# Gate loads on ScalarE's own queue, row sums shifted by two, and a bank of its own for the last quarter of the last products

## The reference

```python
h = layer_norm(x)
z = h @ w_in                                   # pooled channels | q | k | v
mix = concat(pool_mixer(z), window_attention(z)) @ w_o
h = layer_norm(alpha * h + mix)
# product-key retrieval over 128*128 one-neuron experts, 8 heads, 16 picks each
a = einsum('td,thkd->thk', h, u_tab[idx])      # idx: 128 picked experts of a token
w = softmax_gates * gelu(a)
ffn = einsum('thk,thkd->td', w, v_tab[idx])
ple = sigmoid(h @ w_gate + b) * (p @ w_ple)
h = layer_norm(alpha * h + ffn + ple)
```

## Time and profile before

| | us |
|---|---|
| median of 3 runs (lowest, highest) | 1350.71 (1350.45, 1350.95) |
| the profiled execution: its own time | 1351.04 |
| its span, first to last instruction | 1349.1 |
| TensorE busy | 1325.6 |
| VectorE busy | 1158.7 |
| ScalarE busy | 658.0 |
| GpSimd busy | 572.4 |

### The profile page before, as it was taken

How to read it: one execution, slowest core, us unless ns; L and a number is a source line. 1 busy time by engine, 2 the same in 40 slices (tenths; PEclk the granted TensorE clock), 3 DMA queues, 4 the chain that set the end, 5 groups by cost and what they waited for, 6 DMA issues and landing times.

```text
span 1349.1 us, 23150 instructions
## 1 busy us (share of the span) xinstructions
PE 1325.6 (98%) x7689; PEld 719.4 (53%) x7689; DVE 1158.7 (86%) x2286; ACT 658.0 (49%) x928; POOL 572.4 (42%) x344
## 2 busy tenths in 40 slices
PE   6999999999999999999999999999999999999997
PEld 3554555546666666666655555555544444444443
DVE  8665579999988999999778888898998989988887
ACT  5552554546667676767543333343333433333341
POOL 2640233435553343434336666666663433322202
PEclk9999999999999999999999999999999999999999
DMA  7222222326577899999999999999999999999952
GB/s 294 94 79 94 79 94 78 110 78 184 183 235 234 338 375 366 359 376 373 395 337 368 350 374 352 361 399 362 371 365 383 386 391 391 385 389 377 362 185 97
DMA packets 148796, 384.51 MB, mean 285 GB/s; under 512 B 11776, under 2 KB 71424, under 8 KB 146560
## 3 DMA queue, kind: packets, MB, share of 16 engines
q1 hardware_dynamic: 111872, 249.54, 52.4%
q0 software_dynamic: 36864, 134.23, 25.7%
HBM read 340.74 MB, written 42.99 MB: 284 GB/s over the span
## 4 chain that ended last, share of the span: by engine, by line
PE 94%; DVE 3%; ACT 1%; issue 1%; DMA 1%; DVEq 0%; SPq 0%; ACTq 0%
PE bank L658 37%; PE bank L646 16%; PE bank L648 16%; PE bank L647 16%; PE bank L871 2%; PE bank L873 2%; PE bank L673 2%; PE bank L929 1%; PE bank L820 1%; PE bank L600 1%; PE bank L777 1%; PE bank L718 1%; PE bank L696 1%; DVE ple_gate L1766 0%; DMA norm_rows<-norms_dram 0%
## 5 line engine op out<-in xcount | busy, mean ns | idle before, releaser
L658 PE MATMUL bank<-cut,area 128*128 128x512 f16 x2208 | 483.2, 379 | 1.6 <-DVE cut L1324 1.6
L646 PE MATMUL bank<-hT,cut 128*128 128x384 f16 (+1 forms) x1232 | 413.0, 335 | 1.1 <-DVE cut L1324 0.5
L647 PE MATMUL bank<-hT,cut 128*128 128x384 f16 (+1 forms) x1232 | 412.8, 335 | 0.0
L648 PE MATMUL bank<-hT,cut 128*128 128x384 f16 (+1 forms) x1232 | 412.7, 335 | 0.0
L956 ACT ACTIVATE cut<-raw 128x1024 f16<-128x1024 f32 x246 | 256.0, 1054 | 204.5 <-PE bank L658 112.0
L658 PEld LDWEIGHTS bank<-cut,area 128*128 128x128 f16 x2208 | 215.9, 98 | 258.5 <-DVE cut L1324 2.5
L1324 DVE SCALAR_TENSOR_TENSOR cut<-raw,cut 128x1024 f16<-128x1024 f32 x198 | 248.1, 1254 | 63.0 <-ACT cut L956 61.6
L1173 ACT ACTIVATE gelu_out<-bank 128x384 f32<-128x384 f32 x120 | 59.0, 491 | 246.0 <-PE bank L648 246.0
L646 PEld LDWEIGHTS bank<-hT,cut 128*128 128x128 f16 x1232 | 120.6, 98 | 93.4 <-DVE hT L1446 3.0
L582 POOL DMA_INDIRECT ple_sb<-u_rows_dram,expert_id x64 | 112.3, 1755 | 135.6 <-DVE dots_now L1673 103.1
L648 PEld LDWEIGHTS bank<-hT,cut 128*128 128x128 f16 x1232 | 120.6, 98 | 90.9 <-issue 0.3
(11 more groups left out here) (190 smaller groups left out, 1552.3 us busy)
## 6 DMA issues: line engine op xcount, KB each, us to landing
raw<-tiles_dram SPq DMA_DIRECT2D x298, 512.0 KB, 6.4
gates_scratch<-area SPq DMA_DIRECT2D x12, 2048.0 KB, 11.7
area<-gates_scratch SPq DMA_DIRECT2D x32, 768.0 KB, 9.5
gelu_scratch<-gelu_out SPq DMA_DIRECT2D x80, 192.0 KB, 4.9
area<-gelu_scratch SPq DMA_DIRECT2D x20, 768.0 KB, 10.9
norm_rows<-norms_dram SPq DMA_DIRECT2D x3, 1024.0 KB, 5.9
hn<-x_dram SPq DMA_DIRECT2D x4, 512.0 KB, 4.9
out_dram<-hn SPq DMA_DIRECT2D x3, 512.0 KB, 2.6
```

The lines of the kernel that those rows point to most:

```text
L646: nc.tensor.matmul(dst, w[0], hT[:, 0, k, 0:width], start=(k == 0), stop=False)
L647: nc.tensor.matmul(dst, w[0], hT[:, 1, k, 0:width], start=False, stop=False)
L648: last = nc.tensor.matmul(dst, w[1], hT[:, 0, k, 0:width], start=False, stop=(k == KD - 1))
L658: mm = nc.tensor.matmul(bank[:, 2 * tt + h, :], lhs(a)[:, tt * P:(tt + 1) * P], cut[:, t.slot, b, h * HALF:(h + 1) * HALF], start=(first a ...
```

## The change

Four edits:

1. The gate loads of `both` and `late` leave SyncE's program. ScalarE issues them, on a queue of its own, right behind the cut of the weight whose making frees the buffer. The first two gate loads stay with SyncE. SyncE's `load_gelu` gets the wait (on `weight_done`) that the gate load ahead of it had.
2. `EIGHT_SUMS` goes from (24, 24) to (26, 22): e = 3 adds two rows more, e = 4 two less.
3. `light = 2` for e = 4: its first six passes keep three row adds each, its last two have two each.
4. The second half of the last token tile's last products is done as two quarters, the fourth in bank 6 (`2 * ND`), started afresh there. VectorE adds all of bank 5 after the third quarter (what bank 5 holds for the fourth from earlier tiles with it), then 256 columns of bank 6, with statistics of 512, 256 and 256 columns in `last_stats`.

```diff
-EIGHT_SUMS = (24, 24)
+EIGHT_SUMS = (26, 22)
+LAST_PIECES = ((2 * ND - 2, 0, HALF), (2 * ND - 1, HALF, HALF // 2), (2 * ND, HALF + HALF // 2, HALF // 2))
...
@@ SyncE, both(e) @@
-                    if p % 4 == 2:
-                        s = p // 4
-                        if isinstance(e, int) and e == EIGHTS - 1:
-                            load_gates(2 * e + 2 + s, VG * s, s)
-                        else:
-                            load_gates(2 * e + 2 + s, U_EARLY + VG * (2 * e + 2 + s), s)
@@ SyncE, late(e) @@
-                        load_gates(2 * EIGHTS + 2 * e + s + 2, VG * (2 * e + s + 2), s)
+                        sp.wait_ge(weight_done, N_BOTH + VG * (2 * e + s + 1))
                         load_gelu(2 * e + s + 2, s)
@@ TensorE, the last products of the last token tile @@
-            for h in range(2):
+            for piece in LAST_PIECES:
                 for i in range(2 * RING):
-                    mm = last_products(i, ND - 1, (h,))
+                    mm = last_products(i, ND - 1, (piece,))
                 mm.then_inc(experts_done, 1)
@@ ScalarE @@
+            def load_gates(group, first, parity):
+
+                act.wait_ge(weight_done, VG * (group - 1))
+                nc.scalar.dma_start(gates_in[:, parity],
+                                    gates_dram[:, :, bass.ds(first, VG), :].rearrange("c p e t -> p c e t")
+                                    ).then_inc(gates_loaded[parity], 16)
...
                         for w in ((i + 1, i + 2) if i == N_BOTH - 2 else (i + 2,)):
                             weight_high(w, w % RING, v_tile(w - RING))
+                        if p == 6:
+                            load_gates(2 * e + 3, VG, 1)
...
                     weight_high(i + 1, (p + 1) % RING, None if no_use else v_tile(i + 1 - RING))
+                    if p == 2 and isinstance(e, int) and e == EIGHTS - 1:
+                        load_gates(2 * e + 2, 0, 0)
+                    elif p % 4 == 2:
+                        load_gates(2 * e + 2 + p // 4, U_EARLY + VG * (2 * e + 2 + p // 4), p // 4)
...
+                    if v % 4 == 1 and (not fixed or 2 * e + v // 4 + 2 < N_LATE // VG):
+                        load_gates(2 * EIGHTS + 2 * e + v // 4 + 2, VG * (2 * e + v // 4 + 2), v // 4)
@@ VectorE, both(e, step, steps, light=0) @@
-                step_at = [steps * q // 8 for q in range(9)]
+                early = steps - 2 * light
+                step_at = [early * q // (8 - light) for q in range(9 - light)]
+                step_at += [early + 2 * (q + 1) for q in range(light)]
@@ VectorE, the end @@
-            for h in range(2):
-                dve.wait_ge(experts_done, 3 + h)
-                final_half(2, h)
-                final_stats(3, h)
-                if h == 0:
+            for n, (into, begin, count) in enumerate(LAST_PIECES):
+                dve.wait_ge(experts_done, 3 + n)
+                evicted = HALF if n < 2 else count
+                sums_n = hn[:, ND - 1, begin:begin + evicted]
+                nc.vector.scalar_tensor_tensor(out=sums_n, in0=bank[:, into, 0:evicted],
+                                               scalar=1 / (S_G * S_V * ALPHA), in1=sums_n, op0=ALU.mult,
+                                               op1=ALU.add).then_inc(final_sum, 1)
+                dve.wait_ge(final_sum, 2 * 3 + n + 1)
+                own.mark(nc.vector.bn_stats(last_stats[:, 6 * n:6 * n + 6], hn[:, ND - 1, begin:begin + count]))
+                if n == 0:
```

More of the change, by code:

```diff
@@ L191, in layer @@
         gate_b_row = sb("gate_b_row", [P, D])
+        last_stats = sb("last_stats", [P, 6 * len(LAST_PIECES)])
         stats = sb("stats", [P, TT, 12])
@@ L923, in _, with last_products, both_halves @@
             first_weight = N_BOTH + N_LATE - 2 * RING
-            def last_products(i, tt, columns_now):
+            def last_products(i, tt, pieces):
                 for step, (a, b) in enumerate(((0, 0), (0, 1), (1, 0))):
-                    for h in columns_now:
-                        mm = nc.tensor.matmul(bank[:, 2 * tt + h, :],
+                    for into, first, count in pieces:
+                        mm = nc.tensor.matmul(bank[:, into, 0:count],
                                               weight_halves(first_weight + i, i % RING)[:, a, tt * P:(tt + 1) * P],
-                                              halves_of(last[i])[:, b, h * HALF:(h + 1) * HALF],
-                                              start=False, stop=(i == 2 * RING - 1 and step == 2))
-                return mm
+                                              halves_of(last[i])[:, b, first:first + count],
+                                              start=(into == 2 * ND and i == 0 and step == 0),
+                                              stop=(i == 2 * RING - 1 and step == 2))
+                return mm
+            def both_halves(tt):
+                return ((2 * tt, 0, HALF), (2 * tt + 1, HALF, HALF))
             for group in (range(RING), range(RING, 2 * RING)):
@@ L1774, in _, with both @@
             weight_low(0, 0)
-            def both(e, step, steps):
-                step_at = [steps * q // 8 for q in range(9)]
+            def both(e, step, steps, light=0):
+                early = steps - 2 * light
+                step_at = [early * q // (8 - light) for q in range(9 - light)]
+                step_at += [early + 2 * (q + 1) for q in range(light)]
                 for p in range(8):
@@ L1810, in both_dots, with both_sums @@
                 keep_dots(first, count)
-            def both_sums(e, first, count):
+            def both_sums(e, first, count, light):
                 weights_now(first, count)
-                both(e, lambda j: add_row(j, first + j, first // ROW_RING + j // ROW_RING), count)
+                both(e, lambda j: add_row(j, first + j, (first + j) // ROW_RING, (first + j) % ROW_RING), count,
+                     light)
             first = U_GATES + KEPT_DOTS
@@ L1832, in _ @@
             for n, count in enumerate(EIGHT_SUMS):
-                both_sums(len(EIGHT_DOTS) + n, first, count)
+                both_sums(len(EIGHT_DOTS) + n, first, count, 2 if n == len(EIGHT_SUMS) - 1 else 0)
                 first += count
@@ L1855, in final_moments @@
                 own.settle()
-                own.link(nc.vector.bn_aggr(moments[:, t, :], stats[:, t, :]))
+                own.link(nc.vector.bn_aggr(moments[:, t, :], last_stats[:] if i == 3 else stats[:, t, :]))
                 nc.vector.tensor_scalar(v, moments[:, t, 1:2], EPS / ALPHA ** 2, None, ALU.add).then_inc(stats_done, 1)
```

19 lines of the change are left out of this document (8 added, 11 removed).

## The result

| | before | after |
|---|---|---|
| median of the runs | 1350.88 us (1350.45 to 1351.45, 6 runs) | 1360.65 us (1355.89 to 1365.53, 6 runs) |
| profiled execution, its span | 1351.04, 1349.1 us | 1363.67, 1361.8 us |

The ratio is 1.0074, 95% interval 1.0063 to 1.0085. The change makes the kernel about 10 us slower. The profiled execution is one of the slower of the six, so its trace shows 12.7 us more than before. The forecast was 1348.5 us, and the range up to 1350.6 doesn't hold the time. The rival "gates starve on their own queue" had 0.11.

What follows compares the result with a forecast made beforehand. TensorE was taken to bound the kernel, busy 1325.6 of 1349.1 us. The terms -1.76 - 0.09 - 0.40 = -2.25 us took the median from 1350.71 to 1348.5 us; range 1347.6 to 1350.6.

Steps and rivals of the forecast that it cites:

- gates starve on their own queue: Rival: gate loads beside two full queues land late; at 20 us to landing, 6.0 us lost, 1354.5 us; chance 0.11.
- the cost of nothing: Moving gate loads to ScalarE: 0.38 us of issue saved on SyncE each time, worth nothing on the path.
- It took 11.2 us before: 1003.3: Pass 6 of `both(4)`: gate load issued at 992.1 lands at 1003.3, 1.1 us before its use in `late`.
- four turns, 13 us or more: All gate loads except that of pass 6 in `both(4)`: each has four turns, 13 us or more, to land.
- bound of 14 us for the load of pass 6: Gate load of pass 6 in `both(4)`: a landing up to 1006.1, 14 us after issue, stalls nobody.
- Edits 2 and 3, -1.76: TensorE's stall at 1004: two fewer row adds bring VectorE's cut 2.78 us forward, winning 1.76 us.
- That rival's own two cases, 1.1 and 1.8 us: Rival, stall moves to a transfer in `late`: late gates lose 1.1 us, late gelu 1.8; 1349.0 to 1350.3; chance 0.22.
- The -0.09: Matmuls behind the stall at 1004: a hidden 0.09 us won, as the stored gelu is issued and lands sooner.
- Edit 4, -0.40: Tail behind the last matmul: splitting the last half into quarters starts the joining of statistics sooner, winning 0.40 us net.
- + 0.06: Tail: 48 matmuls of 256 columns take 5.24 us instead of 5.18 for 24 of 512, costing 0.06 us.
- The third stall: TensorE near 1323, 0.63 us: forecast to stay, as VectorE waits for norm rows; chance 0.12 that it goes, giving 1347.8.

Runs made afterwards that it cites:

- experiment 1: The changed kernel with the gate loads back on SyncE, row adds and last quarter as changed; 1348.41 us, ratio 0.9979.
- experiment 2: The kernel before with the gate loads issued by ScalarE and nothing else changed; 1364.39 us, ratio 1.0091.
- experiment 3: The changed kernel with ScalarE's gate loads reading 768 KB in runs of 6 KB, always from one place; 1348.23 us, ratio 0.9977.
- experiment 4: The changed kernel with ScalarE's gate loads in runs of 1 KB, always the same bytes; 1348.52 us, ratio 0.9975.
- experiment 5: The changed kernel with ScalarE's gate loads in runs of 256 bytes, always from one place; 1379.32 us, ratio 1.0204.
- experiment 6: The changed kernel with half of each gate load issued by SyncE and half by ScalarE, in runs of 512 bytes; 1348.58 us, ratio 0.9979.
- experiment 7: The kernel before with the row-add changes alone (26 and 22 rows, last two turns light); 1348.72 us, ratio 0.9982.
- exp. 8: The kernel before with only the last products' fourth quarter in a bank of its own; 1350.17 us, ratio 0.9994.
- exp. 12: The changed kernel with the gate loads back on SyncE, run once more on another chip; 1348.00 us, ratio 0.998.
- exp. 9: The changed kernel with gate loads back on SyncE and norm rows loaded ahead of the last tile loads; 1348.16 us, ratio 0.9978.

## Why the prediction was wrong, point by point

**Edit 1, the step that failed.** "It took 11.2 us before: 1003.3": the working took the landing of a load from a queue that it was to leave, and the cost of nothing followed from that. The one load that it worked out harmed nobody: it landed 13.7 us after its issue, and it could take 14. Its cover was indeed the thinnest. (Why it landed so much sooner than the loads before and behind it isn't known.) The others were passed over with "four turns, 13 us or more". The next of them took 23.6 us; VectorE could have borne 16.5 of that and TensorE 19.4 (23.6 less the 4.2 that it lost). In `both`, before any stall, nine loads (issued between 700 and 985) took 12.8 to 29.8 us, and TensorE lost nothing, since 31 us lie between two of them there; in `late` it is 15.5, four tiles of TensorE, where nothing stalls. Experiments 1 and 2 show the whole loss in this edit. Experiments 3 to 6 show its reason, the number of runs of one load in a queue beside two full ones:

| runs for each DMA engine, their size | landing, us (median, longest) | median of those in 700:985 | time, us |
|---|---|---|---|
| 8 of 6 KB | 8.0, 10.0 | 9.1 | 1348.23 |
| 48 of 1 KB | 13.1, 19.8 | 17.9 | 1348.52 |
| 48 of 512 bytes (half of a load) | one at 15.6 | not in the trace | 1348.58 |
| 96 of 512 bytes (the change) | 15.2, 29.8 | 22.6 | 1360.65 |
| 192 of 256 bytes | 42.1 the longest in the chain | not in the trace | 1379.32 |

The last column but one compares best. Behind the first stall the change's landings go up and down, from 24.8 us to 6.7, and that pulls its median down.

Could rows have given the size? Roughly. In 1066:1190 a packet of q1 lasts 0.449 x 16 x 124 / 5359 = 0.166 us, one of q0 in the same way 0.149 and one of q10 0.029. A run that waits for a packet of the tile queue alone takes 0.195, and of both 0.344, so 96 runs take 18.7 to 33 us, as an estimate; measured were 23.6 to 24.8 at those on the path and 29.8 at the longest. It is no strict bound. In the same way, from their own traces, 48 runs of 1 KB come to 17.4 us at most and took up to 19.8, and 8 runs of 6 KB come to 4.6 and took 8.0 at the median: some us come on top that the sum doesn't hold. The trace of before gives the first two durations in much the same size: 0.149 for q0, and 0.458 x 16 x 13 / 655 = 0.145 for the tile queue in 725:738, where it carries no gates. Whether a turn takes one run or several, of every queue alike, the sums are the same and these runs don't tell.

**The rival "gates starve".** Its mechanism, its place (`late`) and its sign were right. Its bound of 14 us for the load of pass 6 was too, as experiment 6 shows, but that load didn't reach it in the changed kernel. Its price was wrong, since it looked at that load alone: 6.0 us at a landing of 20 us, 1354.5. It is six stalls, since a load in three lands late, and a slower pace behind the longest.

**The rules of the Trainium skill.** The sentence of the Trainium skill, "DMA: Bandwidth & Descriptors", section "Issuing engines are not separate DMA queues", that issuing from several engines saves only sequencer time, was put against this change as saying that it does nothing. The issue was indeed all that it saved, 0.38 us a time. But how the transfers of the three queues then interleaved cost 12 us. Another section of that page of the Trainium skill, "Queues, rings and completion order", has each DMA engine go round its queues in turns, and the traces agree so far as that landing grows with the number of runs, 9.1 to 17.9 to 22.6 us at the median in 700:985 for the same bytes. I had it in the text and gave the rival that it stands by 0.11, as no row of before had a third queue.

**Edits 2 and 3, -1.76.** Right, and nothing moved in its place. (That rival's own two cases, 1.1 and 1.8 us on 1348.5, give 1349.6 to 1350.3; its 1349.0 came from neither.) The cut started at 1001.95 against the forecast 1004.84 - 2.78 = 1002.06, the stall is gone in the changed kernel and in experiments 1 and 7, and the passes of four adds stall nobody. The -0.09 wasn't won as such: experiment 7 loses 0.11 us at another place, near 1039, where 11 matmuls from 1037.72 on take 2.65 us and others 2.54.

**Edit 4, -0.40.** A little small. The 24 matmuls of the third quarter, of 256 columns each, took 1351.62 - 1349.00 = 2.62 us, 0.109 each as forecast. The joining of statistics started 0.96 us behind the last matmul's end, where before took 1.49:

```profile
1353.25 0.68 DVE L1944 SCALAR_TENSOR_TENSOR hn<-bank,hn 128x512 f32<-128x512 f32 x1
...
1354.44 0.42 DVE L1944 SCALAR_TENSOR_TENSOR hn<-bank,hn 128x256 f32<-128x256 f32 x1
...
1355.36 0.24 DVE L1871 BATCH_NORM_AGGREGATE moments<-last_stats 128x2 f32<-128x18 f32 x1
```

```profile
1353.91 0.49 PE L922 MATMUL bank<-area 128*128 128x256 f16 x3
```

That is -0.53 + 0.06 = -0.47, and from the last matmul to the end of the span it is 7.4 us, 7.5 forecast.

**The third stall.** "The stall at 1323 stays" holds by its cause, VectorE's wait for the norm rows. The wait shows in the time from the start of the cut ahead of it to the start of the gain that needs the rows, and TensorE's loss follows it from kernel to kernel:

| | before | changed | exp. 1 | exp. 8 | exp. 12 | exp. 7 | exp. 9 |
|---|---|---|---|---|---|---|---|
| cut to gain, us | 1.74 | 1.67 | 1.59 | 1.35 | 1.27 | 1.21 | 1.14 |
| TensorE loses, us | 0.63 | 0.56 | 0.50 | 0.25 | 0.17 | 0.11 | 0.03 |

Experiments 1 and 12 are one kernel, so some 0.3 us of it come and go from run to run, whatever the edit. The profiled span of experiment 1 is 2.8 us under before's in place of 2.25. The 0.55 between are made up by 0.13 of this stall, 0.07 of the tail and 0.38 that it was ahead already at the first of the 90 matmuls of the earlier trace rows, 984.55 in place of 984.93.

## What to carry to other kernels

Beside two full queues, a load's time to landing went by the queue that it stood in and by the number of its runs, more than by its bytes. Before a load moves to a queue of its own beside full ones, count its runs for each DMA engine, multiply by the packet times of the other queues, add a few us, and put that against the cover of every such load, not of the one with the least; here 96 runs needed 23.6 us, and TensorE would have borne 23.6 - 4.2 = 19.4. If the layout gives short runs, leave the load in the queue whose other loads can wait, put only half of it on the new queue, or move a load of long runs instead.

## What the runs showed that I had not expected

- What one queue gains another pays: with the gates gone from SyncE, tile loads landed in 7.2 in place of 9.7 us, and none of that was of use.
- Issuing sooner didn't help: the load at 1001.84 left 8.35 us ahead of its like in the kernel before, and VectorE stood 7.14 us for it. In the kernel before it stood 3.08 us at that turn, for the stored gelu and not for gates.
- Behind the stall of 4 us TensorE's clock fell. In 1028:1034 the mean granted clock is 0.72, a mixture of its two levels, 1.2 and 2.4 GHz: 21 matmuls started where 27.8 would at full pace. The 216 matmuls from there on took 1.68 us more than those of later pieces. The matmuls behind the stalls of 1.3 to 2.3 us ran at the full pace. The rows, with the view's columns as in the earlier trace rows:

```profile
1020.00:1027.00 7.00, 3.87 (x18) 1.56 (x16) 1.33 (x3) 0.74 (x2) 0.00 (x0) 1.00 1.00 341
1028.00:1034.00 6.00, 6.00 (x21) 2.39 (x20) 6.00 (x8) 2.34 (x4) 2.45 (x2) 0.72 0.73 236
```

- An issue can be held. Of ScalarE's 30 issues of 256-byte runs three took 3.6, 4.8 and 9.1 us, where those of 512 bytes never took over 0.45. Why isn't shown.
